# Hybrid diffusion step, attention stage: TensorE turns the next unit's probabilities before it makes the scores three units on

## What is computed

```python
s_lat = einsum('bijqhd,bijkhd->bhijqk', qb, kg) * scale + bias[None]
s_ctx = einsum('bijqhd,bkhd->bhijqk', qb, k_ctx) * scale
p = softmax(concatenate([s_lat, s_ctx], axis=-1), axis=-1)
o = (einsum('bhijqk,bijkhd->bijqhd', p[..., :n_lat], vg)
     + einsum('bhijqk,bkhd->bijqhd', p[..., n_lat:], v_ctx))
# context tokens
s = einsum('bqhd,bkhd->bhqk', qblk, k) * scale
o = einsum('bhqk,bkhd->bqhd', softmax(s), v)
```

## Time and profile before

| what | value |
|---|---|
| median of 3 runs | 4318.09 us (4312.22 to 4319.15) |
| the profiled execution, its own time | 4316.63 us |
| its span in the trace | 4315.0 us |
| TensorE matmul busy | 3882.6 us, 90% of the span |
| VectorE busy | 2562.3 us, 59% |
| ScalarE busy | 1821.1 us, 42% |
| mean granted TensorE clock | 0.948 of full speed |
| attention stage, about | 1118 to 1658 us of the span |
| 1200 to 1300 us, within it | TensorE busy 94.62 us, VectorE 71.31, ScalarE 69.49 |

### The profile page before, as it was taken

How to read it: one execution, slowest core, us unless ns; L and a number is a source line. 1 busy time by engine, 2 the same in 40 slices (tenths; PEclk the granted TensorE clock), 3 DMA queues, 4 the chain that set the end, 5 groups by cost and what they waited for, 6 DMA issues and landing times. The chain is left out here.

```text
span 4315.0 us, 69324 instructions
## 1 busy us (share of the span) xinstructions
PE 3882.6 (90%) x25083; PEld 3405.9 (79%) x25083; DVE 2562.3 (59%) x4875; ACT 1821.1 (42%) x2862; POOL 507.7 (12%) x458
## 2 busy tenths in 40 slices
PE   7899999999799997595996299999999999999992
PEld 3688888888688895595995288888888888888881
DVE  4655554555567766231321767777777777777774
ACT  3511111110576663111113066666666666666663
POOL 0000000000444652000000000000000000000000
PEclk9999999999899998798998699999999999999996
DMA  9434434343544445635325167777777777777776
GB/s 350 139 127 134 133 130 137 127 134 116 136 137 113 119 136 195 222 103 176 112 80 190 54 225 253 255 257 258 258 255 255 254 253 254 255 256 254 253 241 251
DMA packets 568508, 818.44 MB, mean 190 GB/s; under 512 B 23600, under 2 KB 455296, under 8 KB 556544
## 3 DMA queue, kind: packets, MB, share of 16 engines
q1 hardware_dynamic: 545760, 699.64, 50.0%
q0 software_dynamic: 22688, 118.02, 8.5%
HBM read 715.89 MB, written 101.71 MB: 189 GB/s over the span
## 5 line engine op out<-in xcount | busy, mean ns | idle before, releaser
L1758 DVE TENSOR_TENSOR e_wlo<-e_raw,e_whi 128x1024 fp32r<-128x1024 f32 x768 | 905.0, 1219 | 355.5 <-ACT e_whi L1674 352.5
L1899 PE MATMUL ps<-e_xs,e_whi 128*128 128x320 f32 x4096 | 1061.4, 345 | 16.6 <-DVE e_xs L1766 9.0
L1899 PE MATMUL ps<-e_xs,e_wlo 128*128 128x160 f32 x4096 | 934.6, 238 | 0.0
L1674 ACT ACTIVATE e_whi<-e_raw 128x1024 fp32r<-128x1024 f32 x768 | 768.9, 1054 | 386.0 <-DMA e_raw<-in_w_gate 153.2
L1899 PEld LDWEIGHTS ps<-e_xs,e_whi 128*128 128x128 f32 x4096 | 754.8, 188 | 26.5 <-DVE e_wlo L1758 13.9
L1899 PEld LDWEIGHTS ps<-e_xs,e_wlo 128*128 128x128 f32 x4096 | 770.1, 191 | 0.7
L1302 PE MATMUL ps<-o_whi,mhi 128*128 128x256 f32 x1280 | 364.5, 285 | 101.2 <-DMA mlo<-mixlo 101.2
L1917 PE MATMUL ps<-e_whi,e_h 128*128 128x512 f32 x1024 | 405.4, 396 | 7.8 <-DVE e_h L1792 7.8
L484 PE MATMUL ps<-hhi,p_whi 128*128 128x512 f32 (+1 forms) x1536 | 386.6, 360 | 8.5 <-DVE p_wlo L423 8.5
L441 DVE SCALAR_TENSOR_TENSOR p_acc<-p_modraw,cT,p_acc 128x256 f32<-128x256 f32 x960 | 386.4, 478 | 0.6 <-DMA p_modraw<-in_w_mod 0.6
L484 PE MATMUL ps<-hlo,p_whi 128*128 128x512 f32 (+1 forms) x1536 | 383.5, 358 | 0.0
(11 more groups left out here) (237 smaller groups left out, 6037.7 us busy)
## 6 DMA issues: line engine op xcount, KB each, us to landing
e_raw<-in_w_gate SPq DMA_DIRECT2D x64, 2048.0 KB
e_raw<-in_w_up SPq DMA_DIRECT2D x64, 2048.0 KB
e_raw<-in_w_down SPq DMA_DIRECT2D x64, 2048.0 KB
p_modraw<-in_w_mod SPq DMA_DIRECT2D x128, 512.0 KB, 3.7
m_raw<-in_w_mod SPq DMA_DIRECT2D x16, 2048.0 KB, 14.6
p_raw<-in_w_in SPq DMA_DIRECT2D x64, 512.0 KB, 4.8
o_raw<-in_w_out SPq DMA_DIRECT2D x16, 2048.0 KB, 8.8
projT<-p_out_st POOLq DMA_DIRECT2D x32, 640.0 KB, 3.6
```

What stands on the lines that cost most here:

```text
L1674: nc.scalar.activation(piece(whi, c, q), piece(raw, c, q), ACT.Copy).then_inc(w_hi_made, 1)
L1758: nc.vector.tensor_tensor(piece(wlo, c, q), piece(raw, c, q), piece(whi, c, q).bitcast(F32), ALU.subtract).then_inc(w_lo_made, 1)
L1899: last = nc.tensor.matmul(bank[:, 0:cols], w[:, s, at:at + P], xs[:, k, 0:cols], start=(k == 0 and w is whi), stop=(k == KD - 1 and w is whi))
```

## The change

In the loop body of TensorE's stream two calls change places. Nothing else changes: the same instructions run, with the same waits, and the streams of the other engines are as they were.

```diff
             turn(0, 0)
             with pe.Fori(0, J) as j:
                 for u in range(U):
+                    turn(j, u + 1)
                     scores(j, u + 3)
-                    turn(j, u + 1)
                     if u in BATCH_AT:
                         batch(j + (u > W), BATCH_AT[u])
                     values(j, u)
                 turn_last_pair(j)
```

## The result

The changed kernel takes 4353.03 us (median of 4 runs, 4352.59 to 4354.69) against 4316.04 us before (4 runs, 4312.22 to 4319.15). By the medians that is 37 us slower. The ratio is 1.0093, with a 95% interval of 1.0081 to 1.0105, or 35 to 45 us. Its profiled execution took 4352.59 us, with a span of 4351.0.

The account below looks back on a forecast made before the run. It took TensorE as the bound in most bodies, VectorE in turns 15 to 17. Waits of 29.0 us and 7 for the clock on 4316.6 gave 4352.6, median 4354 us; forecast 20 to 60 us slower, range 4328 to 4388.

Parts of the forecast that it names:

- The end of the iteration: At the iteration boundary, TensorE idles before the last pair and next turn: 1.36 us, seven times, and 0.7 after the last.
- The clock: TensorE's clock falls to 1.2 GHz behind the iteration-end gaps: half of seven ends at 2 us, 7 us; bounds 0 to 35.
- The rival with a fall at every end: Half clock at every iteration end, with upper bounds 29 + 35 + 8, gives 4390 us; chance 0.15.
- Turns 3, 6 and 11: Turns in bodies with extras or behind short values wait for ScalarE's copy: 0.53, 0.18 and 0.68 us an iteration.
- the other layings cost nothing: ScalarE's three value layings other than turn 11's have 0.88 us or more to hide in: cost 0, otherwise 0.5 each.
- the plain body: A latent body without extras takes 3.16 us on TensorE; ScalarE's chain still fits, with 0.88 us to spare.
- The pair of turn 19: The pair's transpose in turn 19 is reached sooner and waits for VectorE's output: 0.46 us an iteration.
- the stall: Turns 15 to 17, bound by VectorE: pairs stay put, but scores 19 now come behind turn 17's pair; 0.5 us.
- that of turn 14: The pair in turn 14 has the same 0.46 us wait as turn 19's, but the longer stall below swallows it.
- The first iteration: Costed at 2.35 us, like each of the eight iterations.
- The moved wait: Wait on a sequencer register instruction: taken as 0; upper bound 0.05 us for 152 turns, 8 us.
- The faster rival: VectorE's 2.50 us cast passes outside GpSimd's low keys if starting over 4 us after `k_high`: 4288 us; chance 0.05.

Follow-up runs that it names:

- the fillers: Changed kernel plus 10 unused identity transposes on TensorE ahead of each iteration's last pair and 9 behind it: 4335.70 us, ratio 1.005.
- Body 0 alone: Kernel before, with the new order (turn, then scores) in body 0 of each iteration only: 4325.96 us, ratio 1.003.
- the cast on ScalarE: Kernel before, with each pair's cast (high part) moved from VectorE to ScalarE, behind its copy: 4281.16 us, ratio 0.992.
- the kernel with the cast: Changed order together with each pair's cast moved from VectorE to ScalarE: 4315.67 us, ratio 1.0002 to the kernel before.

## Why the prediction was right, point by point

- **The total** was forecast as 4354 us and is 4353. Part of that is luck. The attention stage lost 41 us, not 36, and in the profiled execution the rest was 5 us shorter; the terms below miss in both directions. My text gives two widths, 20 to 60 us slower and 4328 to 4388 us; the result lies in both.
- **The end of the iteration** (1.36 us, seven times): right. With the clock held by the fillers it is 1.36. Body 0 alone, behind the old body 19, costs 0.90 where the clock holds. The chain of exponentials, batch read and last copy was read to 0.1 us.
- **The clock** (7 us, half of the seven ends at 2 us): right in mechanism. It fell at all seven ends and cost 1.4 us each by the fillers, 10 us. The rival with a fall at every end was right about how often, and not about 5 us each. My half came from a reading of the earlier trace rows that undercounts: in the kernel before, the granted clock between batches 14 and 17 is under 1.00 in all eight iterations (0.65 to 0.89), not in about four. What I left out is that the time at half clock in these bodies moves too; the fillers changed it by another 7 to 8 us.
- **Turns 3, 6 and 11** (0.53, 0.18, 0.68): the turns and the cause are right. By the distance of starts the gaps are about 0.56, 0.45 and 0.76. Turn 6 was mis-sized because `k_high` stands ahead of the statistics of unit 6 on VectorE, and its exponentials start 2.15 us after the last scores matmul, not 1.93.
- **Missed: values 6.** They wait 0.56 us (0.22 before) for the output of unit 5. On VectorE the chain from scores 7 through `stats(7)`, `q_low` and `stats(8)` to that output takes 5.5 us in both kernels (1425.64 to 1431.18 here); turn 5, which TensorE did inside that time, now comes ahead of scores 7, so that there is less to cover it. My step "the other layings cost nothing" looked at ScalarE alone in these bodies.
- **Missed: the plain body**, which became 0.06 us shorter. From values to values the four waits cost 2.06 us together, and the seven bodies without one give back 0.35, so that the stretch's sum is 1.71, near my 1.39.
- **The pair of turn 19** (0.46) and **the stall** (0.5): the sum of 0.96 for bodies 12 to 19 was 0.43. The wait of turn 19 is there, 0.23 idle (I had 0.46), and that of turn 14, which I said would be swallowed, shows as +0.33 between batches 12 and 14. What gave it back in bodies 17 to 19 is the time at half clock, which now ends earlier: they took 6.40 at full clock and up to 7.37 before, and take 6.76 now. The pairs of turns 16 and 17 did not keep their waits either: 2.44 us in place of 1.97, and at most 0.33 behind the first iteration in place of up to 2.25.
- **The first iteration** was costed like the others; it lost 6.7 us, 2.5 of them ahead of batch 1 (23.2 us in place of 20.6). Turn 1 waits there for copy 0 with no scores ahead of it, 2.25 us in place of 1.42, and turn 1 and scores 3 run at half clock behind it. That is not proof that the swap costs these 2.5 us: four kernels with body 0 in the old order took 23.6 to 23.7 us there as well, with turn 1 at half clock, and the kernel before and three others 20.6.
- **The moved wait** (0): right. No plain body is longer.
- **The faster rival** did not come, as its condition said: the cast's order behind `k_high` is the same. What it would bring to lift the block altogether, no run shows: with the cast on ScalarE 34 us were won, and the subtraction was still held up.

## What to carry to other kernels

Where an in-order engine is nearly always busy, put the instruction that waits longest behind the ones that can run, not ahead of them. The place to look is not the plain body, which both orders fit, but the bodies with extras and the loop's boundary. For each wait write down the chain to it, with what stands ahead of it in the other engines' queues, and the work that covers it in either order. Then look at the clock behind each new gap: filling two gaps an iteration with useless transposes won 10 us of clock here, and 17 in all. Taking the casts of the pairs off VectorE won 34; in the one split that GpSimd holds up it was some 1 us of VectorE's time (2.50 + 0.99 against 2.56).

## What the runs showed of the hardware

- Two waits of 1.2 and 1.1 us with one transpose between them brought the clock to its lower level at all seven iteration ends of the changed kernel, and at four of seven with the cast on ScalarE; waits of 0.54 and 1.24 us did so at six of seven. Each fall cost 1.4 to 1.6 us, and 2.6 to 2.8 in the kernel with the cast. Nineteen transposes in the gaps kept it at 1.00.
- A VectorE subtraction with both operands in SBUF is held up by a GpSimd operation just as a cast is: 2.56 us against 0.28 in the same kernel. By the Trainium skill (SBUF — State Buffer, "SBUF: two separate sides") the two engines share a port pair, and the later one blocks until the other is done. The trace agrees: both the cast and the subtraction ended with GpSimd's low keys. The skill does not list the same copy on ScalarE among the blocked. The trace agrees here too: its cast at 1356.99, in the middle of the low keys, took 0.31 us, as it did outside them.
- The same code in bodies 14 to 17 took 14.1 or 17.1 us from one iteration to the next, in one execution, with a mean granted clock of 0.76 or 0.61.
